# Forget gates of the HGRN branch computed beside the memory attention, and projections put ahead of the merges in the HGRN stage

## The reference

```python
def hgrn2_branch(q, f_fwd, f_bwd, i, z, lb, onorm):
    def direction(f_logit, lb_d):
        f = lb_d + (1.0 - lb_d) * jax.nn.sigmoid(f_logit.astype(F32))
        return heads(1.0 - f), heads(jnp.log(f))
    k_f, g_f = direction(f_fwd, lb[0])
    k_b, g_b = direction(f_bwd, lb[1])
    o_fwd = gla_scan(qh, k_f, ih, g_f)
    o_bwd = rev(gla_scan(rev(qh), rev(k_b), rev(ih), rev(g_b)))
    o = rmsnorm(o_fwd + o_bwd, onorm).reshape(B_, S_, BRANCH_W).astype(q.dtype)
    return o * jax.nn.silu(z)
```

## Time and profile before

| | us |
|---|---|
| median of 3 runs | 2412.63 (2411.73 to 2413.72) |
| profiled execution, its own time | 2409.47 |
| its span | 2407.5 |
| TensorE busy | 2218.6 (92%) |
| VectorE busy | 1349.8 (56%) |
| ScalarE busy | 905.0 (38%) |

### The profile page before, as it was taken

The page is one execution under the profiler, slowest core; times in us unless marked ns, Lnnn a source line. Parts: engine busy times, 40 slices in busy tenths (PEclk is TensorE's granted clock), DMA queues, the critical chain, the costliest instruction groups (busy, mean ns, idle before and its releaser), DMA issues. The chain is left out here.

```text
span 2407.5 us, 30205 instructions
## 1 busy us (share of the span) xinstructions
PE 2218.6 (92%) x11296; PEld 1667.5 (69%) x11296; DVE 1349.8 (56%) x2395; ACT 905.0 (38%) x1527; POOL 122.2 (5%) x153
## 2 busy tenths in 40 slices
PE   6899998899997899996999889999989998999997
PEld 4687765566776566663777678888767767788886
DVE  2552446866445565653345586964444456778544
ACT  3521233133232666764333432332333434233223
POOL 0000001200000223220000000000000000000000
PEclk8785999999998899998999989999989999999999
DMA  5220431132324899985332213322423131241313
GB/s 163 85 80 1 115 106 44 56 98 66 106 77 175 294 369 355 370 317 196 118 104 41 66 62 106 101 88 88 145 92 115 56 77 52 74 133 62 110 49 114
DMA packets 218989, 296.45 MB, mean 123 GB/s; under 512 B 48861, under 2 KB 183085, under 8 KB 210617
## 3 DMA queue, kind: packets, MB, share of 16 engines
q1 hardware_dynamic: 213722, 286.09, 35.6%
q0 software_dynamic: 5120, 8.40, 1.1%
HBM read 283.12 MB, written 22.07 MB: 127 GB/s over the span
## 5 line engine op out<-in xcount | busy, mean ns | idle before, releaser
L1581 PE MATMUL acc<-x_hi,w_hi 128*128 128x512 f32 x1432 | 577.9, 404 | 19.7 <-DVE w_lo L1532 16.3
L1582 PE MATMUL acc<-x_lo,w_hi 128*128 128x512 f32 x1432 | 565.7, 395 | 0.0
L1583 PE MATMUL acc<-x_hi,w_lo 128*128 128x512 f32 x1432 | 564.8, 394 | 0.0
L1502 ACT CAST w_hi<-raw 128x1024 fp32r<-128x1024 f32 x179 | 186.9, 1045 | 620.0 <-PE acc L1583 585.3
L1532 DVE TENSOR_TENSOR w_lo<-raw,w_hi 128x1024 fp32r<-128x1024 f32 x174 | 212.8, 1224 | 292.3 <-ACT w_hi L1502 289.3
L1581 PEld LDWEIGHTS acc<-x_hi,w_hi 128*128 128x128 f32 x1432 | 273.4, 191 | 84.6 <-DVE w_lo L1532 17.4
L1583 PEld LDWEIGHTS acc<-x_hi,w_lo 128*128 128x128 f32 x1432 | 272.6, 190 | 59.9
L1582 PEld LDWEIGHTS acc<-x_lo,w_hi 128*128 128x128 f32 x1432 | 273.5, 191 | 58.1 <-issue 2.0
L1186 DVE TENSOR_TENSOR w_lo<-wgu,w_hi 128x1024 fp32r<-128x1024 f32 x128 | 150.7, 1219 | 66.4 <-ACT w_hi L1144 63.0
L1144 ACT CAST w_hi<-wgu 128x1024 fp32r<-128x1024 f32 x128 | 128.0, 1047 | 43.9 <-DMA wgu<-in_moe_w_up 36.9
L1117 PE MATMUL ps<-wd,y 128*64 128x512 f32 x256 | 116.7, 598 | 0.7 <-DVE y L1202 0.7
(11 more groups left out here) (561 smaller groups left out, 3411.2 us busy)
## 6 DMA issues: line engine op xcount, KB each, us to landing
raw<-in_w_in SPq DMA_DIRECT2D x60, 1024.0 KB, 5.6
raw<-in_w_gate SPq DMA_DIRECT2D x40, 1024.0 KB, 5.3
wgu<-in_moe_w_gate SPq DMA_DIRECT2D x32, 1024.0 KB
wgu<-in_moe_w_up SPq DMA_DIRECT2D x32, 1024.0 KB
wd<-in_moe_w_down SPq DMA_DIRECT2D x32, 1024.0 KB
raw_b<-in_w_branch SPq DMA_DIRECT2D x56, 256.0 KB, 2.7
room<-in_w_out SPq DMA_DIRECT2D x3, 2048.0 KB, 8.0
y_t<-in_w_out SPq DMA_DIRECT2D x3, 2048.0 KB, 10.3
```

The lines of the kernel that those rows point to most:

```text
L1502: self.nc.scalar.copy(self.w_hi[n % 2], self.weights(n)).then_inc(self.rounded, 1)
L1581: pe.matmul(acc, hi, tile.hi[:, k, :], start=(k == 0), stop=False)
L1582: pe.matmul(acc, hi, tile.lo[:, k, :], start=False, stop=False)
L1583: mm = pe.matmul(acc, lo, tile.hi[:, k, :], start=False, stop=(k == KT - 1))
```

## The change

The work of the forget gates moves out of the HGRN stage: a new class issues the sigmoid as ScalarE's first instruction of the memory attention stage, the four scalings at VectorE's steps 1 to 4 and the keys at step 5. The logarithm becomes ScalarE's first instruction of the HGRN stage. In that stage the 4 projection tiles now come first and the 8 merge tiles after them, and one tile more stands ahead of `turn_keys(1)`. The big buffers (`wj`, `qm`, `g`, `rel`, `ex`, `ke`, `rest`) become slices of one buffer `planes` of 10 planes. `lb`, the lower bounds of the gates, is fetched beside the window attention. All of it holds for both layers.

```diff
@@ new class, before attention_stage @@
+class ForgetGates:
+    def __init__(self, c, ctx, k, g, lb):
+        self.nc, self.k, self.g, self.lb = c.nc, k, g, lb
+        self.om = c.sb(ctx, "om", [P, 4])
+        self.steps = 0
+        self.sigmoid, self.chain = (c.sem(x) for x in ("sigmoid", "gates_dve"))
+
+    def act(self, act):
+        self.nc.scalar.activation(self.g, self.k, ACT.Sigmoid).then_inc(self.sigmoid, 1)
+
+    def dve_step(self, dve, s):
+        nc, run = self.nc, Chain(dve, self.chain, self.steps)
+        if s == 0:
+            run(nc.vector.tensor_scalar(self.om[:], self.lb, -1.0, 1.0, ALU.mult, ALU.add))
+            dve.wait_ge(self.sigmoid, 1)
+        if 1 <= s <= 4:
+            j = s - 1
+            run(nc.vector.tensor_scalar(self.g[:, j, :], self.g[:, j, :], self.om[:, j:j + 1], self.lb[:, j:j + 1], ALU.mult, ALU.add))
+        if s == 5:
+            run(nc.vector.tensor_scalar(self.k, self.g, -1.0, 1.0, ALU.mult, ALU.add))
+        self.steps += run.n
@@ attention_stage, scalar block @@
             def _(act):
+                if forget is not None:
+                    forget.act(act)
                 if gate is not None and not lead:
                     nc.scalar.activation(th[:], gate, ACT.Tanh, scale=0.5).then_inc(th_ready, 1)
@@ attention_stage, vector block @@
                     att.dve_step(dve, s)
+                    if forget is not None:
+                        forget.dve_step(dve, s)
                     for n in beside[s]:
                         stream.dve(dve, n)
@@ hgrn_stage @@
-def hgrn_stage(c, stream, fill, room, gate, lb, gain, y):
+def hgrn_stage(c, stream, fill, room, planes, gate, gain, y):
-        g = c.sb(ctx, "g", [P, 4, S])
-        cum2, rel, ex, ke = c.sb(ctx, "cum", [P, 2, 2, S]), *(c.sb(ctx, x, [P, 2, S]) for x in ("rel", "ex", "ke"))
+        g, rel, ex, ke = planes[:, 0:4], *(planes[:, n:n + 2] for n in (4, 6, 8))
+        cum2 = c.sb(ctx, "cum", [P, 2, 2, S])
...
                 stream.pe(pe, U[4])
+                stream.pe(pe, U[5])
                 turn_keys(1)
                 products(1)
-                stream.pe(pe, U[5])
+                stream.pe(pe, U[6])
                 updates(1)
                 within(1)
-                stream.pe(pe, U[6])
+                stream.pe(pe, U[7])
                 from_before(1)
...
-                nc.scalar.activation(g[:], k, ACT.Sigmoid).then_inc(sig, 1)
+                nc.scalar.activation(g, g, ACT.Ln).then_inc(logs, 1)
                 stream.act(act, U[0])
-                act.wait_ge(f_ready, 1)
-                nc.scalar.activation(g[:], g[:], ACT.Ln).then_inc(f_ready, 1)
                 stream.act(act, U[1])
                 exponentials(0)
...
-                run(nc.vector.tensor_scalar(om[:], lb, -1.0, 1.0, ALU.mult, ALU.add))
                 run(nc.vector.tensor_scalar(half[:], gain, 0.5, None, ALU.mult))
-                dve.wait_ge(sig, 1)
-                for j in range(4):
-                    run(nc.vector.tensor_scalar(g[:, j, :], g[:, j, :], om[:, j:j + 1], lb[:, j:j + 1], ALU.mult, ALU.add))
-                run(nc.vector.tensor_scalar(k, g[:], -1.0, 1.0, ALU.mult, ALU.add))
-                dve.sem_inc(f_ready, 1)
...
                 stream.dve(dve, U[0])
-                dve.wait_ge(f_ready, 2)
+                dve.wait_ge(logs, 1)
                 arguments(0)
...
                 masked(1)
+                stream.dve(dve, U[6])
                 states(1)
-                stream.dve(dve, U[6])
+                stream.dve(dve, U[7])
                 results(1)
...
@@ second_block @@
-            of_window, of_memory = merge(3, True), merge(4)
-            conv = stream.project(w_in, 1280, 14, x_hi, x_lo)
+            of_window, glu_tiles, of_memory = merge(3, True), stream.project(w_in, 1280, 4, x_hi, x_lo), merge(4)
+            conv = glu_tiles + stream.project(w_in, 1792, 10, x_hi, x_lo)
...
-                    wj, km, qm = c.sb(ctx, "wj", [P, 6, S]), c.sb(ctx, "km", [P, 2, MEM]), c.sb(ctx, "qm", [P, 4, S])
+                    wj, km, qm = planes[:, 0:6], c.sb(ctx, "km", [P, 2, MEM]), planes[:, 6:10]
...
-                    attention_stage(c, stream, [], of_window, units, HD ** -0.5, qm[:, 2:4])
+                    attention_stage(c, stream, [], of_window, units, HD ** -0.5, qm[:, 2:4],
+                                    forget=ForgetGates(c, ctx, h_room[:, 2:6], planes[:, 0:4], lb[:]))
...
-                    hgrn_stage(c, stream, [*of_memory, *conv[0:4]], h_room, gates[:], lb[:], gain[:], y_t[:, 0:2])
-                    rest = c.sb(ctx, "rest", [P, 10, S])
-                    stream.into(conv[4:14], [rest[:, j] for j in range(10)])
+                    hgrn_stage(c, stream, [*conv[0:4], *of_memory], h_room, planes[:], gates[:], gain[:], y_t[:, 0:2])
+                    stream.into(conv[4:14], [planes[:, j] for j in range(10)])
```

More of the change, by code:

```diff
@@ L1982, in hgrn_stage @@
         at, st = c.sb(ctx, "att", [P, 4, NT, CH]), c.sb(ctx, "state", [P, 2, NCH, HD])
-        om, half = c.sb(ctx, "om", [P, 4]), c.sb(ctx, "half_gain", [P, 2])
+        half = c.sb(ctx, "half_gain", [P, 2])
         ps = c.ps(ctx, "ps", [P, 5, 512])
@@ L1990, in hgrn_stage @@
         norm = ChannelNorm(c, ctx, y, c.const("half"), HD, 1e-6, False, rel[:], ps[:, 0:2], ps[:, 4])
-        (sig, f_ready, th_ready, v_turned, v_ready, args, exps, ke_ready, qk_ready, turned, kr_ready, att_done, att_ready,
+        (logs, th_ready, v_turned, v_ready, args, exps, ke_ready, qk_ready, turned, kr_ready, att_done, att_ready,
          upd_done, st_ready, intra_done, o_done, chain) = (c.sem(x) for x in (
-             "sig", "f", "th", "v_turned", "v", "args", "exps", "ke", "qk", "turned", "kr", "att_mm", "att", "upd", "state",
+             "logs", "th", "v_turned", "v", "args", "exps", "ke", "qk", "turned", "kr", "att_mm", "att", "upd", "state",
              "intra", "o", "dve"))
@@ L2074, in _ @@
                 stream.pe(pe, U[4])
+                stream.pe(pe, U[5])
                 turn_keys(1)
                 products(1)
-                stream.pe(pe, U[5])
+                stream.pe(pe, U[6])
                 updates(1)
                 within(1)
-                stream.pe(pe, U[6])
+                stream.pe(pe, U[7])
                 from_before(1)
-                stream.pe(pe, U[7])
+                stream.pe(pe, U[8])
                 norm.pe_sums(pe)
-                stream.pe(pe, U[8])
+                stream.pe(pe, U[9])
                 norm.pe_spread(pe)
-                for n in U[9:]:
+                for n in U[10:]:
                     stream.pe(pe, n)
@@ L2115, in _ @@
                 stream.act(act, U[8])
+                stream.act(act, U[9])
                 norm.act_root(act)
-                for n in U[9:]:
+                for n in U[10:]:
                     stream.act(act, n)
@@ L2212, in _ @@
                 masked(1)
+                stream.dve(dve, U[6])
                 states(1)
-                stream.dve(dve, U[6])
+                stream.dve(dve, U[7])
                 results(1)
                 norm.dve_squares(dve)
-                stream.dve(dve, U[7])
+                stream.dve(dve, U[8])
                 dve.wait_ge(th_ready, 1)
@@ L2220, in _ @@
                 norm.dve_variance(dve)
-                stream.dve(dve, U[8])
+                stream.dve(dve, U[9])
                 norm.dve_inverse(dve)
-                stream.dve(dve, U[9])
+                stream.dve(dve, U[10])
                 norm.dve_scale(dve)
@@ L2227, in _ @@
                                                        ALU.mult, ALU.mult))
-                for n in U[10:]:
+                for n in U[11:]:
                     stream.dve(dve, n)
@@ L3371, in second_block @@
             with ExitStack() as whole:
-                gates = c.sb(whole, "h_gate", [P, 2, S])
+                gates, planes = c.sb(whole, "h_gate", [P, 2, S]), c.sb(whole, "planes", [P, 10, S])
                 gain, lb = c.sb(whole, "gain", [P, 2]), c.sb(whole, "lb", [P, 4])
@@ L3403, in second_block @@
                     stream.into(conv[0:4], [glu[:, j] for j in range(4)])
-                    hgrn_stage(c, stream, [*of_memory, *conv[0:4]], h_room, gates[:], lb[:], gain[:], y_t[:, 0:2])
-                    rest = c.sb(ctx, "rest", [P, 10, S])
-                    stream.into(conv[4:14], [rest[:, j] for j in range(10)])
+                    hgrn_stage(c, stream, [*conv[0:4], *of_memory], h_room, planes[:], gates[:], gain[:], y_t[:, 0:2])
+                    stream.into(conv[4:14], [planes[:, j] for j in range(10)])
                     c.load_beside([(h_room, of("w_out_2")[:, 0:512].rearrange("(k p) n -> p k n", p=P))])
-                    conv_stage(c, stream, [*conv[4:14], *of_rest[0], *of_rest[1], *of_rest[2]], glu[:], rest[:], w31[:], w3[:], cb[:], cg[:], ca[:],
+                    conv_stage(c, stream, [*conv[4:14], *of_rest[0], *of_rest[1], *of_rest[2]], glu[:], planes[:], w31[:], w3[:], cb[:], cg[:], ca[:],
```

5 lines of the change are left out of this document (2 added, 3 removed).

## The result

| | before | changed |
|---|---|---|
| median of 20 runs each, us | 2411.78 (2404.32 to 2416.99) | 2418.7 (2411.34 to 2422.39) |
| ratio | | 1.0034, 95% interval 1.0026 to 1.0042 |
| span of the profiled execution | 2407.5 | 2415.1 |

The change makes the kernel slower, by 8 us by the ratio and by 7 between the two medians. The predicted 2415.8 and its range of 2409 to 2422 hold that time. The likeliest case, within 0.2% of before, does not: the whole interval lies above 1.002, on the side that had a chance of 0.32.

A forecast was written before the change was run, and what follows sets the result against it. TensorE, at 92% of the span, was taken as the bound. Memory attention +6.8 less HGRN 5.2 gives +1.6 us a layer, +3.2 for two; on 2409.47 that is 2412.7, and 3.2 to the median gives 2415.8, range 2409 to 2422.

The forecast's parts named there:

- The likeliest case: Whole kernel: time within 0.2% of before, 2415.8 us with its own range of 2411 to 2418; chance 0.53.
- my sum: Both stages together: memory attention's loss of 6.8 less the HGRN stage's gain of 5.2, +1.6 us a layer.
- 6.8 predicted: Memory attention: loss a layer from head wait 3.7, odd steps 2.4 and slower clock 0.7; between 6.1 and 8.1 us.
- the head wait: Memory attention, after its first tile: TensorE waits 3.7 us for `b_lo` behind ScalarE's table loads and sigmoid.
- The term for the odd steps: Memory attention: VectorE's new work at steps 1, 3 and 5 is not covered and costs 2.4 us a layer.
- gain of 5.2 predicted: HGRN stage: TensorE's loss from waits and slow matmuls falls from 16.9 to 11.7 us a layer.
- the slow stretch behind the keys' wait: HGRN stage, behind the 3.9 us wait ahead of the forward keys: lower clock, 1.8 us of slow matmuls not hidden.
- none behind 1.7 and 2.4: HGRN stage, `br` of `U[4]` and `U[5]`: the clock does not fall behind these waits, 0 us of slow matmuls.
- Layer 1 has the same waits: HGRN stage before the change: layer 1 loses the same as layer 0, including the first wait of 5.70 us.
- The first: Rival: HGRN clock also falls behind 2.4 us ahead of `U[5]`'s `br`, 2.9 us a layer, 2421.6, slower; chance 0.32.
- The second: Rival: VectorE's odd steps hide and neither new wait lowers the clock, -3.3 us a layer, 2406; chance 0.15.
- the rest keeps its time: Kernel outside memory attention and HGRN stage: its time does not change.

The follow-up runs named there:

- e2: Changed kernel with merge tiles first and no extra tile ahead of the backward keys, so the gates move and the planes stay shared; ratio 1.003.
- e11: Changed kernel with only the tile order undone (merge tiles first, then projections), extra tile and moved gates kept; ratio 0.9998.
- e6: Kernel before with one edit, an extra tile ahead of the backward keys; ratio 0.9984.
- e5: Changed kernel without the extra tile ahead of the backward keys; ratio 1.0044.
- e3: Changed kernel with the gates' scalings at VectorE's even steps 2 to 8 and the keys in halves at steps 10 and 12; ratio 1.0008.
- e4: Changed kernel with the sigmoid written as a tanh at the memory attention's head, so no table loads there; ratio 1.0000.
- e7: Changed kernel with the sigmoid as a tanh behind step 1's exponential, scalings at even steps, keys in halves at steps 10 and 12; ratio 0.9970.
- e10: e7 with the real sigmoid at step 1, which needs two table loads there; ratio 0.9986.
- e12: e7 with the merge tiles first and the projections last; ratio 0.9958, median 2403.71 us.
- e8: e7 with the logarithm also moved, behind the last exponential of the memory attention; ratio 0.9966.

## Why the prediction was right in its steps and wrong in its likeliest case

**The parts.** One way from before to the changed kernel, one edit at a time, in us a layer: gates moved (e2 against before) +6.6 - 3.1 = +3.5; extra tile (e11 against e2) -3.9; projections first (changed against e11) +2.4. That such a chain ends at the total, +2.0, proves nothing by itself; my sum was +1.6. The edits depend on each other. The extra tile is worth 3.4 to 3.9 with the merge tiles first (e6 against before, e11 against e2) and 2.0 with the projections first (changed against e5); projections first costs 0.6 without the extra tile and 2.4 with it. The same code of the HGRN stage took 110.8 to 111.9 us with projections first (changed, e3, e4, e7, e10, ten stages) and 109.2 to 110.7 with merge tiles first (e11, e12, four stages), so 2.4 is at the high end; between the means it is 1.7. The prediction saw the change as two stages and had their totals nearly right, but it did not see that one of the three edits, the order of the tiles, works against the other two. Following the order with old durations gave each order its waits; I did not work out the same stage with the merge tiles first.

**Memory attention, 6.8 predicted, 6.4 and 6.8 measured.** In layer 0 the head wait was 3.66 (3.7), the transposes waited 0.95 and 1.63 (0.9 and 1.6), the clock fell partly (0.62). The term for the odd steps, 2.4, was too large: the waits grew by 1.84, and step 1 costs nothing that shows. Layer 1 came to 6.8 by another way, with a low clock ahead of the head wait and a wait of 2.16, so that its agreement is partly luck. e3 and e4 take the terms away: 2.0 us for the odd steps (layer 1), 3.2 and 3.6 for the loads and the slow stretch. e4 took away two loads, and the wait shrank by 2.7 us, twice 1.28 and little more. The Trainium skill's drain of some 1380 ns beside each load (ScalarE: Activation LUTs, What ACT_TABLE_LOAD costs) does not show in either.

**HGRN stage, gain of 5.2 predicted, 4.5 and 4.6 measured: the slow stretch behind the keys' wait was mis-sized.** Right were the 3.94 ahead of the keys (the prediction wrote 3.9, its own steps give 3.8 or less), 1.04 (1.2) ahead of the products, 1.85 (1.7) ahead of `U[4]`'s `br`, none ahead of the backward keys. The prediction put 1.8 us of slow matmuls behind the 3.9. In layer 0 the products took 2.53 us up to the next matmul instead of the 1.50 of before, and `U[2]` 6.96 instead of the 5.66 of `U[3]`: 2.3 us, and nothing covers them, since VectorE waits 6.00 us for the updates behind `U[2]`. That is 0.5 of the missing 0.6 to 0.7. How long this stretch lasts varies: in e10 the same wait of 3.94 was followed by a `U[2]` of 6.21 us, and the stage was 0.8 us shorter.

The step "none behind 1.7 and 2.4" was wrong too. It rested on one wait of 2.22 us with a clock of 1.00 behind it; behind 1.85 the clock went to 0.57 for some 3 us, and the tile was slower by 1.6 us. But that took the place of most of the next wait (0.57, against 2.19 where the clock held in e8), and the distance from one `br` to the next is 9.27 us with the fall and without it. This step cost nothing.

"Layer 1 has the same waits" was not right for the kernel before: its first wait there was 4.07 us, behind a head at the low clock (1.76 us for the transposes of `v`), and not 5.70.

**The rivals.** The first, one fall of the clock more, happened, but behind `U[4]` and not behind `U[5]`, and without its price of 2.9 us. That the time still came out on its side, slower, is not its doing. The second is out for the changed kernel: the odd steps were not hidden, and the clock fell. But e7, in another way, comes out below its time.

**What stays open.** The stages give +4.1 us for both layers, the runs some +8. The rest of the kernel, where the code is the same, took 3.5 us longer in the changed kernel's profiled execution (2008.9 against 2005.4). But those stretches lie between 2004.4 and 2014.3 over all profiled executions, with no order by kernel. Over the 13 changed kernels the ratio gives on average 2 us more than the stages do, from -0.1 to +4.2. No edit can be the reason for all of them: e6 has only the extra tile, and e2 does not have it. The profile of before is one from the low side, its own time 2.3 us under the median of the 20 runs, which is enough for the average. For the changed kernel some 2 us more remain that no run places. My "the rest keeps its time" is therefore not shown, and with the stages alone the change would have come out at +0.17%, in my likeliest case. The time came out 2.9 us above my 2415.8, and the stages explain 0.9 of it.

## What to carry to other kernels

Before moving work under another stage, ask at which instruction of the new place it stands: the same gates cost 6.5 us a layer with the sigmoid at the head and the scalings at odd steps, and nothing with the sigmoid as a tanh behind step 1 and the scalings at even steps. Price each edit of a bundle by itself, the reordering too. Waits of the same sum can cost differently by what stands behind them: slow matmuls ahead of another wait shorten that wait and are free, slow matmuls that the next engine waits for are paid in full. Compare TensorE's busy time of the same matmuls, and then the place of the next matmul that waits for another engine.
